# Modulation weights in row blocks, small loads after the caches, and expert loads through the ring alone

## What is computed

```python
def layer(x, mod, P, l, ctx=None):
    sh1, sc1, g1, sh2, sc2, g2 = jnp.split(mod, 6, axis=-1)
    h = rms_norm(x, P["norm_attn_pre"][l]) * (1 + sc1) + sh1
    a, new_ctx = token_mix(h, P, l, ctx)
    x = x + g1 * rms_norm(a, P["norm_attn_post"][l])
    h = rms_norm(x, P["norm_ffn_pre"][l]) * (1 + sc2) + sh2
    x = x + g2 * rms_norm(moe(h, P, l), P["norm_ffn_post"][l])
    return x, new_ctx
```

```python
hid = (jax.nn.silu(jnp.einsum("nd,edf->nef", x, P["moe_w_gate"][l]))
       * jnp.einsum("nd,edf->nef", x, P["moe_w_up"][l]))
routed = jnp.einsum("nef,efd->nd", hid * gates[:, :, None], P["moe_w_down"][l])
```

## Time and profile before

| | |
|---|---|
| time, median of 3 runs | 1754.84 us (1752.04 to 1755.06) |
| the profiled execution's own time | 1753.79 us |
| its span, first to last instruction | 1752.0 us |
| TensorE busy | 1679.8 us, 96% of the span |
| VectorE, ScalarE, GpSimd busy | 431.1, 321.6, 120.0 us |
| moved by DMA | 559.88 MB, mean 320 GB/s |
| the chain that ended last | TensorE 91%, DMA 4%, VectorE 3% |
| the chain's largest lines | L1081 25%, L637 14%, L1109 13%, L1132 12% |

### The profile page before, as it was taken

How to read it: one execution, slowest core, us unless ns; L and a number is a source line. 1 busy time by engine, 2 the same in 40 slices (tenths; PEclk the granted TensorE clock), 3 DMA queues, 4 the chain that set the end, 5 groups by cost and what they waited for, 6 DMA issues and landing times.

```text
span 1752.0 us, 20948 instructions
## 1 busy us (share of the span) xinstructions
PE 1679.8 (96%) x8091; PEld 900.7 (51%) x8091; DVE 431.1 (25%) x1178; ACT 321.6 (18%) x754; POOL 120.0 (7%) x161
## 2 busy tenths in 40 slices
PE   4999998989999999999989999999899999999996
PEld 3878787643333333333367878784333333333332
DVE  1115443351111111111131444433311111111112
ACT  1010341021111111111120113302111111111111
POOL 3001000020000000001010000001100000000000
PEclk9999998999999999999999999899999999999998
DMA  9994232397999999999999633236879999999991
GB/s 354 418 388 161 88 105 70 139 363 302 367 424 426 426 424 425 425 426 425 418 394 404 226 109 105 85 108 253 341 288 414 426 425 425 425 423 425 426 426 80
DMA packets 60781, 559.88 MB, mean 320 GB/s; under 512 B 12972, under 2 KB 13120, under 8 KB 20240
## 3 DMA queue, kind: packets, MB, share of 16 engines
q1 hardware_dynamic: 45504, 528.50, 73.6%
q0 software_dynamic: 15184, 30.07, 5.0%
HBM read 576.02 MB, written 4.78 MB: 332 GB/s over the span
## 4 chain that ended last, share of the span: by engine, by line
PE 91%; DMA 4%; DVE 3%; issue 1%; ACT 1%; SPq 0%; POOL 0%; POOLq 0%; DVEq 0%; ACTq 0%; PEldq 0%
PE PS L1081 25%; PE PS L637 14%; PE PS L1109 13%; PE PS L1132 12%; PE PS L539 6%; PE PS L875 5%; PE PS L923 3%; DMA ring<-in_blocks 2%; PE PS L588 2%; PE PS L655 2%; PE PS L702 2%; PE PS L861 1%; DMA h_table<-region 1%; PE PS L765 1%; PE PS L820 1%
## 5 line engine op out<-in xcount | busy, mean ns | idle before, releaser
L1081 PE MATMUL PS<-ring,region 128*64 128x512 f32 x1920 | 425.6, 596 | 2.7 <-issue 1.5
L1081 PEld LDWEIGHTS PS<-ring,region 128*64 128x64 f32 x1920 | 138.8, 138 | 275.8 <-issue 275.7
L637 PE MATMUL PS<-region,ring 128*128 128x256 f32 x1088 | 245.2, 381 | 0.0
L1132 PE MATMUL PS<-region 128*128 128x512 f32 x512 | 241.0, 594 | 0.0
L637 PEld LDWEIGHTS PS<-region,ring 128*128 128x128 f32 x1088 | 203.8, 190 | 33.5 <-issue 6.3
L1109 PE MATMUL PS<-ring,region 128*64 128x512 f32 x960 | 219.2, 598 | 0.2
L1794 DVE SCALAR_TENSOR_TENSOR region<-region,PS 128x256 f32<-128x256 f32 x64 | 27.0, 421 | 673.4 <-ACT region L1363 673.4
L539 PEld LDWEIGHTS PS<-const,region 128*128 128x128 f32 (+1 forms) x925 | 106.9, 141 | 133.8 <-issue 75.7
L539 PE MATMUL PS<-const,region 128*128 128x128 f32 (+1 forms) x925 | 138.2, 279 | 31.4 <-DMA region<-in_c 11.9
L1109 PEld LDWEIGHTS PS<-ring,region 128*64 128x64 f32 x960 | 63.5, 136 | 147.5 <-issue 146.9
L1367 ACT ACTIVATE region<-PS 128x512 f32<-128x512 f32 x128 | 76.4, 597 | 265.7 <-PE PS L1109 265.7
(11 more groups left out here) (259 smaller groups left out, 1047.4 us busy)
## 6 DMA issues: line engine op xcount, KB each, us to landing
ring<-in_expert_blocks SPq DMA_DIRECT2D x180, 2048.0 KB, 16.2
ring<-in_blocks SPq DMA_DIRECT2D x120, 1024.0 KB, 17.4
region<-in_expert_blocks SPq DMA_DIRECT2D x8, 2048.0 KB, 16.3
region<-in_expert_blocks SPq DMA_DIRECT2D x8, 1024.0 KB, 16.4
region<-post_rows POOLq DMA_DIRECT2D x8, 512.0 KB, 8.3
h_table<-region POOLq DMA_DIRECT2D x4, 512.0 KB, 10.6
region<-in_w_kvk POOLq DMA_DIRECT2D x2, 640.0 KB, 14.0
region<-in_mla_w_ukv POOLq DMA_DIRECT2D x2, 512.0 KB, 18.0
```

The source lines that it names most:

```text
L637: last = pe.matmul(PS[:, j % 2, m * T:(m + 1) * T], w[:, k, m * P:(m + 1) * P], hT[:, k, :], start=(k == 0), stop=(k == KC - 1))
L1081: last = pe.matmul(PS[e * CAP:(e + 1) * CAP, 0, :], xe[:, k, e * CAP:(e + 1) * CAP], w[:, k % 4, :], start=(k == 0), stop=(k == KC - 1), s ...
L1132: last = pe.matmul(PS[:, 4 + 2 * t + half, :], hot[:, t * P:(t + 1) * P], og[:, half * HALF:(half + 1) * HALF], start=False, stop=True, sk ...
```

## The change

1. A modulation block holds 256 rows of 1024 columns instead of 1024 rows of 256 columns. `mod_batch` takes the four blocks of a batch up one by one: it waits for one, runs two steps of the contraction with it, and frees it. The number and the shapes of the matmuls stay.
2. In layer 0 the 16 transposes of the normalised rows stand between batch 0 and batch 1, in layer 1 where they were.
3. GpSimd loads only the identity (128 columns) at the start; the other 1348 columns of constants come after layer 0's caches, with a semaphore `tables_in` that TensorE waits for ahead of the cached keys. `sink`, `rbias`, `lamc` and the lambdas' vectors come after the caches too, in both layers, and count in `lam_loaded`. GpSimd issues layer 0's `prow` loads ahead of its wait for x. VectorE's two small operations on them (`nsink`, `subl`) move from ahead of the first modulation to ahead of the lambdas.
4. The spares are gone: all 32 pairs use the ring, the sync queue's part is one loop that waits for `ring_free` alone, and the router's and the shared expert's tensors are laid elsewhere in `region`.

Cut to its core (the views' new addresses, the removed helpers of the spares and the semaphores' declarations are left out):

```diff
-SPARE_PAIRS = (2, 17)
-PASS_ROUNDS = (EXPERT_LOADS - 6 * len(SPARE_PAIRS)) // RING_SLOTS
+PASS_ROUNDS = EXPERT_LOADS // RING_SLOTS
...
-                def experts_pass(base, q):
-
-                    for n in range(0, 8, 2):
-                        load_expert(n, n // 6, n % 6 // 2, base)
-                    sp.wait_ge(merged_ready, (l + 1) * KC)
-                    load_spare(SPARE_PAIRS[0], 0)
-                    sp.wait_ge(xn_tr, (l + 1) * 8)
-                    load_spare(SPARE_PAIRS[0], 1)
-                    load_expert(8, 1, 1, base)
-                    sp.wait_ge(state_out, (l + 1) * 6 * 16)
-                    sp.wait_ge(router_done, (l + 1) * 2)
-                    sp.wait_ge(shared_gu, (l + 1) * 2)
-                    load_spare(SPARE_PAIRS[0], 2)
-                    load_expert(10, 1, 2, base)
-                    load_pairs(3, 14, 12, base)
-                    sp.wait_ge(spare_used, sp.snap(q * 2) + 1)
-                    for part in range(3):
-                        load_spare(SPARE_PAIRS[1], part)
-                    load_pairs(18, 14, 8 * RING_SLOTS, base)
+                def experts_pass(base):
+                    with sp.Fori(0, PAIRS // 2) as i:
+                        for u in range(2):
+                            for part in range(3):
+                                load_expert(6 * u + 2 * part, i * 2 + u, part, base + i)
...
-            pool.dma_start(const[:], a["consts"]).then_inc(consts_in, 16)
+            pool.dma_start(ident, a["consts"][:, 0:P]).then_inc(consts_in, 16)
...
-            pool.wait_ge(start_tr, 1)
-            apart(pool)
-            pool.wait_ge(x_in, 32)
-            pool.sem_inc(x_ready, 2)
...
-                pool.dma_start(sink[:], at_layer(a["swa_sink"], l).broadcast_to([P, A_HEADS])).then_inc(params_in, 16)
-                pool.dma_start(rbias[:], at_layer(a["router_bias"], l).broadcast_to([P, N_EXPERTS])).then_inc(params_in, 16)
-                pool.dma_start(lamc[:], at_layer(a["lam_consts"], l).broadcast_to([P, 2])).then_inc(params_in, 16)
+                if l == 0:
+                    pool.wait_ge(start_tr, 1)
+                    apart(pool)
+                    pool.wait_ge(x_in, 32)
+                    pool.sem_inc(x_ready, 2)
...
-                    for g in range(MOD_BATCH):
-                        arrived(L_MOD[batch] + g)
-                    for k in range(KC):
-                        for g in range(MOD_BATCH):
-                            w = slot_cols(L_MOD[batch] + g, 256)
-                            last = pe.matmul(PS[32 * g:32 * g + 32, MOD_BANK[group], half * 256:half * 256 + 256], condT[:, k, :], w[:, k, :],
-                                             start=(k == 0), stop=(k == KC - 1), skip_group_check=True)
-                            if k == 0 and g == 0 and frees:
-                                release(last, frees)
-                            if k == KC - 1 and (half == 0 or g < 3):
-                                release(last)
+                    for b in range(MOD_BATCH):
+                        arrived(L_MOD[batch] + b)
+                        w = ring[:, (L_MOD[batch] + b) % RING_SLOTS, :].rearrange("p (k n) -> p k n", k=2)
+                        for k in range(2 * b, 2 * b + 2):
+                            for g in range(4):
+                                last = pe.matmul(PS[32 * g:32 * g + 32, MOD_BANK[group], half * 256:half * 256 + 256], condT[:, k, :],
+                                                 w[:, k % 2, 256 * g:256 * g + 256], start=(k == 0), stop=(k == KC - 1), skip_group_check=True)
+                                if k == 0 and g == 0 and frees:
+                                    release(last, frees)
+                        if half == 0 or b < 3:
+                            release(last)
...
                 def cached_keys():
 
+                    pe.wait_ge(tables_in, 16)
                     pe.wait_ge(caches_in, (l + 1) * 7 * 16)
...
-                dve.wait_ge(params_in, (l + 1) * 9 * 16)
-                step(ve.tensor_scalar(nsink[:], sink[:], -1.0, None, ALU.mult))
-                step(ve.tensor_scalar(subl[:], parT[:, 67:68], lamc[:, 1:2], None, ALU.mult))
...
-                dve.wait_ge(lam_loaded, (l + 1) * 4 * 16)
+                dve.wait_ge(lam_loaded, (l + 1) * 7 * 16)
+                step(ve.tensor_scalar(nsink[:], sink[:], -1.0, None, ALU.mult))
+                step(ve.tensor_scalar(subl[:], parT[:, 67:68], lamc[:, 1:2], None, ALU.mult))
...
-            for g in range(MOD_BATCH):
-                put(L_MOD[batch] + g, w["w_mod"][l][:, 256 * (MOD_BATCH * batch + g):256 * (MOD_BATCH * batch + g + 1)])
+            for b in range(MOD_BATCH):
+                put(L_MOD[batch] + b, w["w_mod"][l][256 * b:256 * (b + 1), 1024 * batch:1024 * (batch + 1)])
```

105 lines of the change are left out of this document (40 added, 65 removed).

## The result

| | before | with the change |
|---|---|---|
| time, median of 5 runs on one chip | 1755.06 us (1752.04 to 1758.82) | 1742.55 us (1741.85 to 1743.64) |
| ratio, 95% interval | | 0.9919 (0.9896 to 0.9942) |
| profiled execution's span | 1752.0 us | 1740.2 us |
| mean granted TensorE clock | 0.986 | 0.988 |
| TensorE busy | 1679.8 us | 1676.8 us |

A second set of runs gives the same ratio, 0.9920 (0.9896 to 0.9945). In it the 15 executions of the kernel before spread from 1747.0 to 1760.6 us, at mean granted clocks of 0.991 for the fastest and 0.983 for the slowest, and the six of the changed kernel only from 1739.8 to 1743.5 us: the fastest of each are 7.2 us apart, the medians 12.5. How much of the gain of the median is clock that the kernel before loses in some of its executions, its one profile doesn't tell.

What follows compares the result with a forecast made beforehand. TensorE bounds the expert pass, with DMA also full; DMA waits bound the pass entries and the start. Savings 1.2 + 2.1 + 3.2 + 0 + 0.45 = 6.95 us off 1753.8 give 1747 us; forecast's range 1744 to 1750, wider 1741 to 1760.

Steps and rivals of the forecast that it cites:

- The expert pass: Both layers' expert passes: removing the spares costs nothing; slowest landing 25.1 us, under the 26.7 us allowed.
- my own sign: Expert pass: the forecast is right if the gate-up's loads land within at most 25 us.
- The slower rival: Expert passes: the spares' lead is real, TensorE waits 11.6 us a pass, time 1770 us; chance 0.13.
- The entries: Entry to each expert pass: without the spares' traffic the first gate-up starts 1.2 us (layer 0) and 2.1 us (layer 1) earlier.
- my own list: Signs that the forecast is right, among them the last table write ahead of the expert pass under 5.5 us.
- The first gate-ups' clock: First gate-up of each pass: shorter idle time ahead holds the clock, saving 1.67 + 1.56 = 3.2 us.
- The start of layer 0: Layer 0's first projections: block 14's landing at 55.2 us bounds the start, gain 0, kept between -1.7 and +2 us.
- the bytes ahead of block 14 stay the same: Layer 0's start: moved tables, lambdas, sinks and biases stay ahead of 55 us, so at most 1.1 us is gained.
- not bound by block 14: Layer 0's start: batch 1 ends at 28.3 us instead of 34.50, all 6.2 us stay, time 1741 us; chance 0.07.
- The start of layer 1: Layer 1's start: VectorE ends the wait and is quicker by two small moved instructions, 0.45 us; row blocks gain nothing.
- the range from 1741: Whole kernel: the range from 1741 to 1760 us leaves out the slower rival and little else.

Runs made afterwards that it cites:

- loads_as_before: The changed kernel with all small loads and the tables where they were before the change (part 3 undone); span 1743.8 us, ratio to before 0.9969.
- smalls_last: The changed kernel with its seven small broadcasts issued still later, once the fourth query projection is copied out; span 1738.1 us, ratio to before 0.9950.
- columns: The changed kernel with modulation blocks by columns and layer 0's transposes behind batch 1 again (parts 1 and 2 undone); span 1742.5 us, ratio to before 0.9950.
- vector_early: The changed kernel with `nsink`, `subl` and their two loads ahead of the first modulation again; span 1744.0 us, ratio to before 0.9948.
- changed_again: The changed kernel run and profiled once more, unaltered; span 1741.7 us, ratio to before 0.9920.

## Why the prediction was right or wrong

**The expert pass: right.** I costed the removal of the spares at nothing; the pass takes 488.03 us with and without the other parts, the idle DMA stretch is filled, and the last landings are up to 24.6 us in layer 0 and 25.5 in layer 1 against the 25.1 that I had worked out (four pairs at 0.44 us make 1.8 and not 1.6, so 25.3). That is over the 25 us of my own sign and still under 26.7: the margin is 1.2 us. The slower rival (1770 us) fell. The rule of the Trainium skill that stood beside it, in "DMA: Bandwidth & Descriptors", section "Rules for kernel authors" (issue early, compute, wait late), is not refuted: the early loads did come early, but the ring had no use for the lead, and their traffic stood beside the table's write.

**The entries: right in sum, with a term mis-sized.** 1.2 and 2.1 us were forecast, 1.22 and 1.87 measured. The last table write did not fall to 5.0 us but to 6.8 and 6.6; what I had missed is that the gather also becomes quicker, 3.5 us instead of 4.55 in layer 0. By my own list a write over 5.5 us would have spoken against the step; in layer 0 the list bound the entry anyway.

**The first gate-ups' clock: right.** 1.67 and 1.56 us were forecast, 1.62 and 1.51 came (8.71 and 8.60 less 7.09).

**The start of layer 0: wrong, 3.6 us instead of 0.** The step that failed is "the bytes ahead of block 14 stay the same". The mechanism was right: loads_as_before waits 1.35 us for block 14 at 56.3 us, exactly as I had argued. In the changed kernel block 14 is used 1.4 us after it lands, so there TensorE's own chain is the later of the two. What came out otherwise is the landing: the change moves what the small broadcasts cost from ahead of block 14 to behind it. I had only asked whether they are issued ahead of 55 us, and not when they are carried out: before, they land from 29.0 to 36.8 us, ahead of blocks 9 to 14, now from 47.6 to 54.1 us, behind caches and tables on their own queue, when block 13 is in. Most of the cost then falls on the blocks behind 14: block 14 lands at 51.3 us, and at 50.8 in smalls_last, where they come after it altogether, a difference smaller than that between the two profiles of the changed kernel (51.3 and 50.5). And I had priced them by bytes. The seven broadcasts carry 169 KB (five of 128 x 64, one of 128 x 8 and one of 128 x 2 floats), 0.4 us at 424 GB/s; they delayed block 20 by 2.8 us (71.0 against 68.2 in smalls_last), and a dip to 180 GB/s stood in the windows of before, in a stretch that I had not looked at. Why they cost so much is open. Their rows are as small as those of two cache loads that cost next to nothing (393 GB/s from 36 to 40 us); what sets them apart is that all 128 rows read the same row of memory, and no run tries them with rows of their own. The rival "not bound by block 14" had given 6.2 us; measured are 3.6, with 1.7 of the difference lost to the clock ahead of the first projection and the rest to the chain.

**The start of layer 1: right in its term, short by the clock.** 0.45 us was forecast and 0.49 found (14.54 us from batch 0 to the projection against 15.03). The projection's 1.69 us was not: I had noted that 1.00 us of idle time left it at full pace and 1.95 us did not, and had not applied it to the 2.02 us here. It needs both the short wait of batch 1 (columns: none gained) and VectorE's 0.45 us (loads_as_before, vector_early: none gained), and in changed_again it failed to come. Without it the first profile would have shown 10.1 us.

**The sum.** 6.95 us forecast; 3.55 for layer 0's start and 1.69 for layer 1's clock added, and 0.3 taken off the entries and gate-ups, make the 11.8 of the spans to 0.1. This is an account of two executions; the 1.69 us are partly luck, since the clock held there in 7 of 10 profiles with this idle time, and the 12.5 us between the medians are not accounted for in this way. The median of the second set, 1741.60 us, lies in the range from 1741; the ratio of 0.9919 against the first median of 1754.84 us gives 1740.6, just below it.

## What to carry to other kernels

Price a small load beside a saturated stream from windows of the trace in which such a load is carried out, not by its bytes: a broadcast of one row to 128 partitions cost several times its bytes here, loads of the same shape with different rows next to nothing. And ask of each moved load which large ones now land ahead of it. An early load into spare space is worth its time only if no idle transfer time follows it; look for that stretch before costing its removal. Removing one wait leaves the next bound close by (block 14 at 51.3 us against a use at 52.7, block 20 at 71.0 against 71.25), so that two halves of a change must be tested together and apart.
